# Squares summed on VectorE, a first round of four tiles, and a last norm through PSUM in a six-layer fp32 block chain

## The chip, the cores and the metric

The kernel runs on one core of a Trainium2 chip. A core has a matrix engine (TensorE, PE in the profile; PEld is its weight load), VectorE (DVE), ScalarE (ACT), GpSimd (POOL) and a queue engine for transfers (SyncE, SP). Data lie in SBUF; matrix products arrive in PSUM, in eight banks of 512 fp32 columns. The metric is the device time of one launch in microseconds (us), the median of several runs.

## What is computed

A chain of residual blocks over 512 tokens of width 1024, all in fp32. The first half has a hybrid mixer, a convolution mixer and two gated MLPs. The second half, where the change lies, is this (each branch is normed before and after):

```python
for i in range(2):
    h = rmsnorm(x, norm_mixer_pre[i])
    m = diff_attention(h, ...) if i == 0 else short_conv(h, ...)
    x = x + rmsnorm(m, norm_mixer_post[i])
    h = rmsnorm(x, norm_mlp_pre[i])
    x = x + rmsnorm(square(relu(h @ w_up)) @ w_down, norm_mlp_post[i])
# rmsnorm(x, g) = x * rsqrt(mean(x * x) + 1e-6) * g
```

## The kernel before

Activations are kept transposed: channels on the 128 partitions, the 512 tokens along the row. A vector of 1024 channels is eight blocks (k = 0 to 7, `KB` = 8) of 128 x 512. `h` is the residual stream, `m` the output of the current branch.

**Tiles.** Each weight matrix is streamed as tiles of 128 x 1024. Tile n goes to slot n mod 4 (`RING` = 4) of `raw`; ScalarE makes its rounded part `whi` (`split_hi`, L290), VectorE the rest `wlo` (`split_lo`, L684), and TensorE multiplies in three passes, (whi, xh), (whi, xl), (wlo, xh), over the eight blocks: 24 matmuls of 512 columns for one tile, all at L1283, into PSUM bank j. `xh` and `xl` are the same split of the activations. The slot of tile n is split for tile n + 4 once tile n is done and, on VectorE, its result has been taken out of PSUM.

**Boundaries.** Between a branch and the next one lie four post-norms: attention to the first MLP ("da" to "mlp0"), first MLP to short convolution ("mlp0" to "sc"), short convolution to second MLP ("sc" to "mlp1"), and the last one, whose result is the output. At each, the squares of `m` are summed (GpSimd adds them into `acc`, TensorE sums over the partitions with a matrix of ones, L1334 and L1336), ScalarE makes `rrow` = rsqrt of it with Ln and Exp (L313, L315), and then for each block k VectorE computes m = m * g * rrow (L705) and h = h + m (L709), ScalarE computes xh = h * g' and the square of h (L303, L299), and VectorE xl = h * g' - xh (L690, `pre_lo`) one block later. GpSimd adds those squares into `acc` too (`sum_squares`, a copy at L1193 and adds at L1196), for the norm of the branch that follows.

**First round.** TensorE's first tiles of the branch that follows don't wait for all of `h`: `first_round` runs three tiles (`FIRST` = 3) together, block by block, each block when its `xl` is there (`x_ready`); all three end with block 7. Its first passes are at L1364, L1365 and L1368. Then comes `row_sum` (L1339, the sum of the squares for the next `rrow`), then the fourth tile alone, then all others by `tile`. What is scaled by the new `rrow` is only the result of a tile, so tiles can run ahead of it as far as PSUM banks and weight slots go.

**After the first round** the MLP's VectorE clears `m` (L1107), waits for `rrow`, and for every tile does relu and scale (`mr`, L1114), a square (`mh`, L1117), the rest `yl` (L1123, after ScalarE's `yh`, L644) and then the split of the next weights. In the short convolution VectorE only scales the tile (L696) before the split.

**Last norm.** `post_norm("mlp1")` on VectorE does m for all blocks and h for the odd ones; GpSimd adds the even ones (L1273). SP stores each block when it is done.

The order on every engine is the order of the code; engines meet only at semaphores.

Of the kernel before, what the change touches and what calls it, by code (L numbers as in the profile page):

```python
# [102 lines left out]
def build(nc, x_t, stream, w_glr, w_gate, vecs, consts, out_t):  # L103
    with ExitStack() as ctx:
# [136 lines left out]

        BY_PE = ("hyb", "da_post", "mlp0_post", "sc_post", "mlp1_post")
        ACC, at = {}, 0
        for n in SUM:
            if n != "lnvar":
                ACC[n] = at
                at += KB - (n in BY_PE)
        PRE = {"hyb": 0, "ff0": 1, "pw": 2, "ff1": 3, "da": 4, "mlp0": 5, "sc": 6, "mlp1": 7}
        POST = {"da": 0, "mlp0": 1, "sc": 2, "mlp1": 3}


        @block.sync
        def _(sp):
            for name in CREDITED:
                sp.sem_inc(s(name), CREDIT)
            sp.dma_start(vec[:], vecs).then_inc(small_in[0], 16)
            sp.dma_start(A["wgr"][:], w_glr).then_inc(s("wglr_in"), 16)
            for k in range(KB):
                sp.dma_start(h[:, k], x_t[k * P:(k + 1) * P, :]).then_inc(x_in[k], 16)
            for j in range(RING):  # L260
                if j == 2:
                    sp.dma_start(const[:], consts).then_inc(small_in[1], 16)
                    sp.dma_start(A["wg2"][0:17, :], w_gate).then_inc(small_in[2], 16)
                sp.dma_start(raw[:, j], stream[j]).then_inc(loaded[j], 16)

            with sp.Fori(1, NT // RING) as r:
                for j in range(RING):
                    sp.wait_ge(wlo_ready, r * RING + (j + 1 - RING))
                    sp.dma_start(raw[:, j], stream[bass.ds(r * RING + j, 1)].rearrange("a p c -> (a p) c"))\
                      .then_inc(loaded[j], 16)  # L270
            for k in range(KB):
# [10 lines left out]
        def _(act):  # L282
# [22 lines left out]

            def inv_rms(name, n, preload=True, bank=4):

# [6 lines left out]
                act.wait_ge(ln_ready, SUM[name] + 1)  # L314
                act.activation(rrow[:], lnb[:], ACT.Exp, scale=-0.5).then_inc(rrow_ready, 1)  # L315

# [306 lines left out]
            def to_m(t0, which):  # L623

                act.preload_act_table_set(LN_EXP)
                for k in range(KB):
# [3 lines left out]
                    split_hi(t)  # L630
                inv_rms(which + "_post", D, preload=False)

# [3 lines left out]
            def mlp(f, t0):  # L636
                name = f"mlp{f}"
                inv_rms(name, D)

# [37 lines left out]
        def _(dve):  # L677
# [19 lines left out]

            def post_norm(which):

                a = POST[which]  # L700
                following = {"da": "mlp0", "mlp0": "sc", "sc": "mlp1"}.get(which)
                dve.wait_ge(rrow_ready, SUM[which + "_post"] + 1)
                for k in range(KB):
                    q = 8 * a + k
                    dve.scalar_tensor_tensor(A["m"][:, k], A["m"][:, k], col("post", q), rrow[:], ALU.mult,  # L705
                                             ALU.mult).then_inc(post_t, 1)
                    if following or k % 2:
                        dve.wait_ge(post_t, q + 1)
                        dve.tensor_tensor(h[:, k], h[:, k], A["m"][:, k], ALU.add).then_inc(h_added, 1)  # L709
# [390 lines left out]
            for k in range(KB):  # L1100
                set_m(Tile(T_DO + k), k)
            post_norm("da")

            def mlp(f, t0):
# [32 lines left out]
                for k in range(KB):  # L1137
                    add_to_m(Tile(t0 + 56 + k), k)
                post_norm(name)

            mlp(0, T_MLP0)


# [33 lines left out]
            for k in range(KB):  # L1177
                set_m(Tile(T_SCO + k), k)
            post_norm("sc")
            mlp(1, T_MLP1)  # L1180


        @block.gpsimd
        def _(pool):
# [82 lines left out]
            with pool.Fori(1, 4) as pair:  # L1267
                pair_inputs(pair)
            for name in ("da_post", "mlp0", "mlp0_post", "sc", "sc_post", "mlp1", "mlp1_post"):
                sum_squares(name)  # L1270
            for k in range(0, KB, 2):
                pool.wait_ge(post_t, 8 * POST["mlp1"] + k + 1)
# [4 lines left out]
        def _(pe):  # L1277
# [52 lines left out]
            def row_sum(name, bank=4):  # L1330
# [6 lines left out]
                else:  # L1337
                    pe.wait_ge(acc_ready, ACC[name] + KB)
                    mm = pe.matmul(ps[:, bank], cst("ones"), acc[:], start=True, stop=True)  # L1339
# [15 lines left out]

            def first_round(t0, hi, lo, hi_ready, ready, base):

                pe.wait_ge(wlo_ready, t0.plus(FIRST - 1).count)
                pe.wait_ge(evac_done, t0.count - 1)
                w_h = [whi[:, j].rearrange("p (k n) -> p k n", k=KB) for j in range(FIRST)]  # L1360
                w_l = [wlo[:, j].rearrange("p (k n) -> p k n", k=KB) for j in range(FIRST)]
# [5 lines left out]
                for j in range(FIRST):  # L1367
                    pe.matmul(ps[:, j], w_h[j][:, 0], lo[:, 0], start=False, stop=False)  # L1368
                for k in range(1, KB):
                    pe.wait_ge(ready, base + (k + 1))  # L1370
                    for j in range(FIRST):
# [242 lines left out]
            mm.then_inc(sum_ready, 1)  # L1614
            first_round(Tile(T_PW2), yh, yl, yh_ready, y_ready, Y0["pw"])
            for j in range(FIRST, KB):
# [298 lines left out]
```

## Time and profile before

| | |
|---|---|
| time, median of 3 runs | 2538.07 us (2537.42 to 2538.41) |
| span of the profiled execution, first to last instruction | 2539.4 us (no other time of it is given) |
| TensorE busy | 94% of the span, 10332 matmuls |
| VectorE, ScalarE, GpSimd busy | 55%, 35%, 13% |
| mean granted clock of TensorE | 0.970 |
| transfers | 82 GB/s over the span |

The profile gives, for each instruction, its start, its length, and in brackets the idle time of its engine just before it with what ended that. The chain of waits is the path that ended last, followed back from the end. TensorE is the engine that is nearly always busy; the stretches in which it is not are the boundaries above. Matmuls overlap, so the time that one costs is the distance between starts, not its length.

### The profile page before, as it was taken

Reading aid. Unit: us, or ns where it says so; the run is one execution under the profiler, and the core shown is the slowest. Engines: PE = TensorE matmul, PEld = TensorE weight load, DVE = VectorE, ACT = ScalarE, POOL = GpSimd, SP = SyncE. Lnnn points to the kernel's source line nnn. Section 1 sums busy time; section 2 is a strip of 40 time slices with the busy share of each in tenths; the row PEclk is TensorE's granted clock in tenths of the full one; section 3 lists DMA queues with packets and bytes.
Section 4 is the critical chain, followed back from the end, with each engine's and each line's share of the span. In section 5 each row is a group of like instructions: output and inputs, shape, how many; then the busy total and the mean of one; then the engine's idle time right before and its main releaser. Section 6 shows DMA issues by size and latency. Waiting matters only on the chain.

```text
span 2539.4 us, 29423 instructions
## 1 busy us (share of the span) xinstructions
PE 2394.7 (94%) x10332; PEld 1886.7 (74%) x10332; DVE 1399.7 (55%) x1630; ACT 877.7 (35%) x1180; POOL 325.5 (13%) x263
## 2 busy tenths in 40 slices
PE   7999999999967589999999999899999899899997
PEld 6867788888744358888887666688888688688885
DVE  4344443444799955444454764845544754844554
ACT  4256432322534344232242444422222322422222
POOL 1001200000456510000012221200001101100002
PEclk9999999999987789999999999999999999999998
DMA  4211233333311113333233110233333233233331
GB/s 163 83 50 34 67 99 100 91 99 99 92 42 41 33 34 107 97 94 99 91 116 92 42 42 28 80 108 100 91 100 95 79 92 99 70 97 100 99 91 50
DMA packets 58129, 208.53 MB, mean 82 GB/s; under 512 B 6449, under 2 KB 6594, under 8 KB 57922
## 3 DMA queue, kind: packets, MB, share of 16 engines
q1 hardware_dynamic: 58050, 207.42, 27.2%
q8 instruction: 56, 0.92, 0.1%
q14 instruction: 23, 0.19, 0.0%
HBM read 205.30 MB, written 2.10 MB: 82 GB/s over the span
## 4 chain that ended last, share of the span: by engine, by line
PE 58%; DVE 6%; ACT 1%; issue 1%; POOL 0%; ACTq 0%
PE ps L1283 53%; PE ps L1650 2%; DVE h L709 1%; DVE m L705 1%; DVE xl L690 1%; DVE wlo L684 1%; PE ps L1673 1%; PE ps L1652 1%; ACT whi L290 1%; PE ps L1611 0%; PE ps L1663 0%; PE ps L1680 0%; DVE cv L933 0%; ACT sq L299 0%; DVE m L1097 0%
## 5 line engine op out<-in xcount | busy, mean ns | idle before, releaser
L1283 PE MATMUL ps<-xh,whi 128*128 128x512 f32 x1767 | 703.6, 398 | 16.8 <-DVE xl L690 13.8
L1283 PE MATMUL ps<-xl,whi 128*128 128x512 f32 x1767 | 689.9, 390 | 0.0
L1283 PE MATMUL ps<-xh,wlo 128*128 128x512 f32 x1767 | 689.9, 390 | 0.0
L684 DVE TENSOR_TENSOR wlo<-raw,whi 128x1024 fp32r<-128x1024 f32 x380 | 482.0, 1269 | 265.8 <-ACT whi L290 254.9
L290 ACT ACTIVATE whi<-raw 128x1024 fp32r<-128x1024 f32 x380 | 398.6, 1050 | 486.4 <-PE ps L1283 486.3
L1283 PE MATMUL ps<-yh,whi 128*128 128x512 f32 x1117 | 437.1, 391 | 0.0
L1283 PE MATMUL ps<-yl,whi 128*128 128x512 f32 x1117 | 434.8, 389 | 0.0
L1283 PE MATMUL ps<-yh,wlo 128*128 128x512 f32 x1117 | 434.8, 389 | 0.0
L1283 PEld LDWEIGHTS ps<-xh,whi 128*128 128x128 f32 x1767 | 333.4, 189 | 101.7 <-DVE xl L690 23.1
L1283 PEld LDWEIGHTS ps<-xl,whi 128*128 128x128 f32 x1767 | 333.1, 189 | 72.0 <-issue 5.1
L1283 PEld LDWEIGHTS ps<-xh,wlo 128*128 128x128 f32 x1767 | 332.9, 188 | 70.4
L1283 PEld LDWEIGHTS ps<-yh,whi 128*128 128x128 f32 x1117 | 210.0, 188 | 44.6 <-issue 1.0
L1283 PEld LDWEIGHTS ps<-yh,wlo 128*128 128x128 f32 x1117 | 209.9, 188 | 43.9
L1283 PEld LDWEIGHTS ps<-yl,whi 128*128 128x128 f32 x1117 | 209.9, 188 | 43.7 <-issue 0.7
L1193 POOL COPY acc<-sq 128x512 f32<-128x512 f32 x12 | 8.0, 668 | 1527.0 <-ACT sq L299 1527.0
L1091 DVE TENSOR_TENSOR m<-ps,m 128x512 f32 (+1 forms) x64 | 44.3, 692 | 183.7 <-PE ps L1283 183.7
L1196 POOL TENSOR_TENSOR acc<-acc,sq 128x512 f32<-128x512 f32 x79 | 113.4, 1436 | 206.4 <-ACT sq L299 205.7
L644 ACT ACTIVATE yh<-mr 128x512 f32 x64 | 40.5, 633 | 225.3 <-DVE mr L1114 225.3
L1586 PE MATMUL ps<-ub,dg 128*128 128x512 f32 x96 | 62.0, 814 | 59.4 <-issue 35.2
L1231 POOL TENSOR_TENSOR pa<-pa,pr 128x512 f32<-128x512 f32 x64 | 99.0, 1547 | 5.0
L489 ACT ACTIVATE yh<-th 128x512 f32 x44 | 27.8, 632 | 205.6 <-DVE th L873 205.6
L1114 DVE SCALAR_TENSOR_TENSOR mr<-ps,rrow 128x512 f32<-128x512 f32 x64 | 44.2, 691 | 96.6 <-PE ps L1283 94.3
(214 smaller groups left out, 2197.7 us busy)
## 6 DMA issues: line engine op xcount, KB each, us to landing
raw<-stream SPq DMA_DIRECT2D x384, 512.0 KB, 3.5
h<-x_t SPq DMA_DIRECT2D x8, 256.0 KB, 5.5
out_t<-h SPq DMA_DIRECT2D x8, 256.0 KB, 2.1
const<-consts SPq DMA_DIRECT2D x1, 1089.0 KB, 9.6
wgr<-w_glr SPq DMA_DIRECT2D x1, 512.0 KB, 3.7
vec<-vecs SPq DMA_DIRECT2D x1, 212.0 KB, 2.6
wg<-w_gate SPq DMA_DIRECT2D x1, 17.0 KB
```

What stands on the lines that cost most here:

```text
L290: act.activation(whi[:, a.slot], raw[:, a.slot], ACT.Copy).then_inc(whi_ready, 1)
L489: act.activation(block_of(yh, i * 2 + u), A["th"][:, u], ACT.Copy).then_inc(yh_ready, 1)
L644: act.activation(block_of(yh, i * 4 + j), A["mr"][:, j % 2], ACT.Square).then_inc(yh_ready, 1)
L684: dve.tensor_tensor(wlo[:, a.slot], raw[:, a.slot], whi[:, a.slot].bitcast(F32), ALU.subtract)\
L690: dve.scalar_tensor_tensor(xl[:, k], h[:, k], col("pre", 8 * PRE[name] + k), xh[:, k].bitcast(F32), ALU.mult, ALU.subtract).then_inc(x_rea ...
L1091: dve.tensor_tensor(block_of(A["m"], k), ps[:, t.slot], block_of(A["m"], k), ALU.add)\
L1114: dve.scalar_tensor_tensor(A["mr"][:, j % 2], ps[:, t.slot], 0.0, rrow[:], ALU.max, ALU.mult)\
L1196: pool.tensor_tensor(acc[:], acc[:], sq[:, k % 2], ALU.add).then_inc(acc_ready, 1)
L1231: pool.tensor_tensor(A["pa"][:, u], A["pr"][:, u * prods % 4] if m == 1 else A["pa"][:, u], product, ALU.add).then_inc(s("cv_padd"), 1)
L1283: mm = pe.matmul(out, lhs, rhs, start=first and n == 0, stop=last and n == 2)
L1586: mm = pe.matmul(ps[:, 5 + u], A["dg"][:, u, k], A["ub"][:, u, k:k + T], start=k == 0, stop=k == TAPS_PE - 1)
L1650: pe.matmul(ps[:, b, 0:kv], A["dq"][r, e, 0, u * P:(u + 1) * P], A["dq"][r, e, 1, 0:kv], start=True, stop=True)
```

## The change

- `post_norm` sums the squares of `h` on VectorE (`sq_sum`), for "mlp0", "sc" and "mlp1": seven adds, the first of two squares at once, in place of GpSimd's copy and seven adds. GpSimd keeps the squares of `m`. `square_block` waits for the new count.
- `first_round` takes the number of tiles (4 in these three branches), keeps blocks 6 and 7 for the end (`tail` = 1) and runs them tile by tile, so that the four tiles end one after the other; `row_sum` follows the second of them.
- The explicit loads of ScalarE's function table in `to_m` (four) and before Ln at "mlp0", "sc" and "mlp1" (three) are gone.
- The last norm is a function of its own: ScalarE writes `rrow` into PSUM bank 5, VectorE reads it there, writes the scaled m of five blocks into PSUM banks 6 and 7 and adds it to h from there; GpSimd adds the other three blocks (0, 3, 6) instead of four.

```diff
@@ square_block
-                    act.wait_ge(acc_ready, ACC[name] + k - 1)
+                    act.wait_ge(acc_ready, ACC[name] + (max(k - 2, 1) if name in BY_DVE else k - 1))
@@ to_m
-                act.preload_act_table_set(LN_EXP)
...
-                inv_rms(which + "_post", D, preload=False)
+                inv_rms(which + "_post", D, preload=False, out=ps[:, 5] if which == "mlp1" else None)
@@ VectorE
+            def sq_sum(name, k):
+                dve.wait_ge(sq_ready, SQ[name] + k + 1)
+                if k == 1:
+                    dve.wait_ge(sum_ready, SUM[name])
+                    dve.tensor_tensor(acc[:], sq[:, 0], sq[:, 1], ALU.add).then_inc(acc_ready, 1)
+                else:
+                    dve.wait_ge(acc_ready, ACC[name] + k - 1)
+                    dve.tensor_tensor(acc[:], acc[:], sq[:, k % 2], ALU.add).then_inc(acc_ready, 1)
@@ post_norm, in the loop over k
-                    if following and k:
+                    if k:
                         pre_lo(following, k - 1)
-                if following:
-                    pre_lo(following, KB - 1)
+                    if k >= 2:
+                        sq_sum(following, k - 1)
+                pre_lo(following, KB - 1)
+                sq_sum(following, KB - 1)
+            def last_norm():
+                a = 8 * POST["mlp1"]
+                dve.wait_ge(rrow_ready, SUM["mlp1_post"] + 1)
+                for k in range(KB):
+                    n = LAST_DVE.index(k) if k in LAST_DVE else 0
+                    if n >= 2:
+                        dve.wait_ge(h_added, 8 * 3 + n - 1)
+                    t = A["m"][:, k] if k in LAST_POOL else ps[:, 6 + n % 2]
+                    dve.scalar_tensor_tensor(t, A["m"][:, k], col("post", a + k), ps[:, 5], ALU.mult,
+                                             ALU.mult).then_inc(post_t, 1)
+                    if k in LAST_DVE:
+                        dve.wait_ge(post_t, a + k + 1)
+                        dve.tensor_tensor(h[:, k], t, h[:, k], ALU.add).then_inc(h_added, 1)
@@ first_round
-                for k in range(1, KB):
+                for k in range(1, KB - 1 - tail):
                     pe.wait_ge(ready, base + (k + 1))
-                    for j in range(FIRST):
+                    for j in range(tiles):
+                        passes(ps[:, j], w_h[j][:, k], w_l[j][:, k], hi[:, k], lo[:, k], False, False)
+                for j in range(tiles):
+                    for k in range(KB - 1 - tail, KB):
+                        if j == 0:
+                            pe.wait_ge(ready, base + (k + 1))
                         mm = passes(ps[:, j], w_h[j][:, k], w_l[j][:, k], hi[:, k], lo[:, k], False, k == KB - 1)
-                        if k == KB - 1:
-                            mm.then_inc(tile_done, 1)
+                    mm.then_inc(tile_done, 1)
+                    if name and j == 1:
+                        row_sum(name)
@@ mlp on TensorE ("sc" likewise)
-                first_round(Tile(t0), xh, xl, xh_ready, x_ready, 8 * PRE[name])
-                row_sum(name)
-                tile(Tile(t0 + FIRST), FIRST, xh, xl)
+                first_round(Tile(t0), RING, xh, xl, xh_ready, x_ready, 8 * PRE[name], name, 1)
```

Two places, as the instructions stand in the program. VectorE at the boundary from "mlp0" to "sc", from the add of block 2, before:

```order
L709 TENSOR_TENSOR h<-h,m 128x512
L690 SCALAR_TENSOR_TENSOR xl<-h,vec,xh 128x512
L705 SCALAR_TENSOR_TENSOR m<-m,vec,rrow 128x512
L709 TENSOR_TENSOR h<-h,m 128x512
L690 SCALAR_TENSOR_TENSOR xl<-h,vec,xh 128x512
L705 SCALAR_TENSOR_TENSOR m<-m,vec,rrow 128x512
```

and now:

```order
L720 TENSOR_TENSOR h<-h,m 128x512
L693 SCALAR_TENSOR_TENSOR xl<-h,vec,xh 128x512
L706 TENSOR_TENSOR acc<-sq 128x512
L717 SCALAR_TENSOR_TENSOR m<-m,vec,rrow 128x512
L720 TENSOR_TENSOR h<-h,m 128x512
L693 SCALAR_TENSOR_TENSOR xl<-h,vec,xh 128x512
L709 TENSOR_TENSOR acc<-acc,sq 128x512
L717 SCALAR_TENSOR_TENSOR m<-m,vec,rrow 128x512
```

One add of squares now stands between the `xl` of a block and the m of the next but one.

VectorE at the last norm, from the last tile's evacuation, before:

```order
L1091 TENSOR_TENSOR m<-ps,m 128x512 x4
L705 SCALAR_TENSOR_TENSOR m<-m,vec,rrow 128x512 x2
L709 TENSOR_TENSOR h<-h,m 128x512
L705 SCALAR_TENSOR_TENSOR m<-m,vec,rrow 128x512 x2
L709 TENSOR_TENSOR h<-h,m 128x512
```

and now:

```order
L1119 TENSOR_TENSOR m<-ps,m 128x512 x4
L737 SCALAR_TENSOR_TENSOR m<-m,vec,ps 128x512
L737 SCALAR_TENSOR_TENSOR ps<-m,vec,ps 128x512
L741 TENSOR_TENSOR h<-ps,h 128x512
L737 SCALAR_TENSOR_TENSOR ps<-m,vec,ps 128x512
L741 TENSOR_TENSOR h<-ps,h 128x512
L737 SCALAR_TENSOR_TENSOR m<-m,vec,ps 128x512
```

Every instruction of VectorE now has one operand in PSUM, and five adds of h stand on it instead of four.

## Rows read from the trace of the kernel before

**Rows 1.** Chain of waits at "mlp0" to "sc": start us, us, what.
```profile
1971.22 0.76 DVE m L705
...
1993.68 4.39 PE ps L1283 x18
1998.07 0.86 PE ps L1339 x2
1998.93 157.84 PE ps L1283 x696
```

**Rows 2.** VectorE and GpSimd there, in order of time: start us, us, instruction.
```profile
1977.46 0.74 DVE L690 SCALAR_TENSOR_TENSOR xl<-h,vec,xh 128x512 fp32r<-128x512 f32 x1
1978.12 0.74 DVE L705 SCALAR_TENSOR_TENSOR m<-m,vec,rrow 128x512 f32<-128x512 f32 x1
...
1978.89 1.85 POOL L1196 TENSOR_TENSOR acc<-acc,sq 128x512 f32<-128x512 f32 x1 [1.91 <-ACT sq L299]
1978.89 0.69 DVE L709 TENSOR_TENSOR h<-h,m 128x512 f32<-128x512 f32 x1
...
1979.50 1.78 DVE L690 SCALAR_TENSOR_TENSOR xl<-h,vec,xh 128x512 fp32r<-128x512 f32 x1
```

**Rows 3.** TensorE's restart there, in order of time.
```profile
1973.60 0.77 PE L1364 MATMUL ps<-xh,whi 128*128 128x512 f32 x1 [3.71 <-ACT xh L303]
1974.16 0.63 PE L1365 MATMUL ps<-xh,wlo 128*128 128x512 f32 x1
1974.59 0.63 PE L1364 MATMUL ps<-xh,whi 128*128 128x512 f32 x1
```

**Rows 4.** Stretches of 1 us: busy by engine; PEclk is the third last number.
```profile
40.00:41.00 1.00, 1.00 (x3) 0.78 (x3) 1.00 (x2) 0.00 (x0) 0.00 (x0) 0.50 0.00 0
...
1613.00:1614.00 1.00, 0.62 (x2) 0.07 (x1) 1.00 (x2) 0.29 (x1) 0.13 (x1) 0.86 0.00 0
...
1978.00:1979.00 1.00, 0.75 (x3) 0.67 (x4) 0.97 (x3) 0.82 (x2) 0.11 (x1) 0.74 0.00 0
```

**Rows 5.** TensorE's restart at "da" to "mlp0", and from the sum to the fifth tile.
```profile
1609.74 0.64 PE L1364 MATMUL ps<-xh,whi 128*128 128x512 f32 x1 [3.71 <-ACT xh L303]
...
1632.27 3.47 DVE L1107 MEMSET m<- 128x4096 f32 x1 [0.80 <-issue]
...
1634.05 1.02 PE L1339 MATMUL ps<-acc,const 128*128 128x512 f32 x2
...
1636.84 0.69 DVE L1114 SCALAR_TENSOR_TENSOR mr<-ps,rrow 128x512 f32<-128x512 f32 x1 [1.10 <-ACT rrow L315]
...
1639.29 1.23 DVE L684 TENSOR_TENSOR wlo<-raw,whi 128x1024 fp32r<-128x1024 f32 x1
...
1640.57 0.50 PE L1283 MATMUL ps<-xh,whi 128*128 128x512 f32 x1
```

**Rows 6.** The same in "sc": ScalarE's Ln and VectorE's first split.
```profile
1998.96 0.60 ACT L313 ACTIVATE lnb<-ps 128x512 f32<-128x512 f32 x1 [4.46 <-PE ps L1339]
...
2001.21 1.23 DVE L684 TENSOR_TENSOR wlo<-raw,whi 128x1024 fp32r<-128x1024 f32 x1
```

**Rows 7.** Two idle spells of TensorE elsewhere, in order of time.
```profile
39.47 0.52 PE L1283 MATMUL ps<-xh,whi 128*128 128x512 f32 x1 [1.92 <-DVE gk L733]
...
1545.84 0.66 PE L1663 MATMUL ps<-const,da 128*128 128x128 f32 x4 [1.71 <-DVE da L1045]
```

**Rows 8.** VectorE at the last norm: its first and its last rows there.
```profile
2524.75 1.42 DVE L705 SCALAR_TENSOR_TENSOR m<-m,vec,rrow 128x512 f32<-128x512 f32 x2 [3.17 <-ACT rrow L315]
...
2535.18 1.64 DVE L709 TENSOR_TENSOR h<-h,m 128x512 f32<-128x512 f32 x1
```

**Rows 9.** VectorE and GpSimd in the convolution mixer, in order of time.
```profile
816.39 0.68 DVE L941 TENSOR_TENSOR cv<-ps,cv 128x512 f32 x1
...
816.87 1.27 POOL L1231 TENSOR_TENSOR pa<-pr 128x512 f32<-128x512 f32 x1 [10.32 <-ACT pr L523]
...
816.99 1.69 DVE L943 TENSOR_TENSOR odd<-pa,odd 128x512 f32<-128x512 f32 x1
```

More of the change, by code:

```diff
@@ L242, in build @@
         BY_PE = ("hyb", "da_post", "mlp0_post", "sc_post", "mlp1_post")
+        BY_DVE = ("mlp0", "sc", "mlp1")
+        ADDS = {n: KB - (n in BY_PE or n in BY_DVE) for n in SUM if n != "lnvar"}
         ACC, at = {}, 0
[L244 to L247, printed above, removed]
+        for n in ADDS:
+            ACC[n] = at
+            at += ADDS[n]
         PRE = {"hyb": 0, "ff0": 1, "pw": 2, "ff1": 3, "da": 4, "mlp0": 5, "sc": 6, "mlp1": 7}
         POST = {"da": 0, "mlp0": 1, "sc": 2, "mlp1": 3}
+        SQ = {n: (SUM[n] - (SUM[n] > 3)) * KB for n in SUM if n != "lnvar"}
+        LAST_POOL = (0, 3, 6)
+        LAST_DVE = tuple(k for k in range(KB) if k not in LAST_POOL)
         @block.sync
@@ L304, in pre_block, with inv_rms @@
                 square_block(name, k, h[:, k])
-            def inv_rms(name, n, preload=True, bank=4):
+            def inv_rms(name, n, preload=True, bank=4, out=None):
                 if preload:
@@ L314, in inv_rms @@
                 act.wait_ge(ln_ready, SUM[name] + 1)
-                act.activation(rrow[:], lnb[:], ACT.Exp, scale=-0.5).then_inc(rrow_ready, 1)
+                act.activation(rrow[:] if out is None else out, lnb[:], ACT.Exp, scale=-0.5).then_inc(rrow_ready, 1)
             def inv_rms_col(n, bank=5):
@@ L696, in scaled, with post_norm @@
                 dve.tensor_tensor(dst, ps[:, bank], rrow[:], ALU.mult).then_inc(evac_done, 1)
-            def post_norm(which):
+            def sq_sum(name, k):
[6 more added lines that the diff above has]
+                    dve.tensor_tensor(acc[:], acc[:], sq[:, k % 2], ALU.add).then_inc(acc_ready, 1)
+            def post_norm(which, following):
                 a = POST[which]
-                following = {"da": "mlp0", "mlp0": "sc", "sc": "mlp1"}.get(which)
                 dve.wait_ge(rrow_ready, SUM[which + "_post"] + 1)
@@ L1101, in _ @@
                 set_m(Tile(T_DO + k), k)
-            post_norm("da")
+            post_norm("da", "mlp0")
             def mlp(f, t0):
@@ L1178, in _ @@
                 set_m(Tile(T_SCO + k), k)
-            post_norm("sc")
+            post_norm("sc", "mlp1")
             mlp(1, T_MLP1)
+            last_norm()
         @block.gpsimd
@@ L1268, in _ @@
                 pair_inputs(pair)
-            for name in ("da_post", "mlp0", "mlp0_post", "sc", "sc_post", "mlp1", "mlp1_post"):
+            for name in ("da_post", "mlp0_post", "sc_post", "mlp1_post"):
                 sum_squares(name)
-            for k in range(0, KB, 2):
+            for k in LAST_POOL:
                 pool.wait_ge(post_t, 8 * POST["mlp1"] + k + 1)
@@ L1354, in col_sum, with first_round @@
                 mm.then_inc(colsum_ready, 1)
-            def first_round(t0, hi, lo, hi_ready, ready, base):
-                pe.wait_ge(wlo_ready, t0.plus(FIRST - 1).count)
+            def first_round(t0, tiles, hi, lo, hi_ready, ready, base, name=None, tail=0):
+                pe.wait_ge(wlo_ready, t0.plus(tiles - 1).count)
                 pe.wait_ge(evac_done, t0.count - 1)
-                w_h = [whi[:, j].rearrange("p (k n) -> p k n", k=KB) for j in range(FIRST)]
-                w_l = [wlo[:, j].rearrange("p (k n) -> p k n", k=KB) for j in range(FIRST)]
+                w_h = [whi[:, j].rearrange("p (k n) -> p k n", k=KB) for j in range(tiles)]
+                w_l = [wlo[:, j].rearrange("p (k n) -> p k n", k=KB) for j in range(tiles)]
                 pe.wait_ge(hi_ready, base + 1)
-                for j in range(FIRST):
+                for j in range(tiles):
                     pe.matmul(ps[:, j], w_h[j][:, 0], hi[:, 0], start=True, stop=False)
```

29 lines of the change are left out of this document (13 added, 16 removed).

## The prediction

> **What bounds the kernel now.** I read the chain of waits first. It is TensorE's tiles nearly throughout: after "mlp0" to "sc", for instance, 696 matmuls run in one piece of 157.84 us, 0.227 us each [rows 1]. What is not TensorE is the boundaries. There the chain starts with the first m (1971.22, call such a start T) and comes back to TensorE only at 1993.68, T + 22.5, with the last 18 of the first round's matmuls, then the sum of squares (done at 1998.93, T + 27.7), then the fourth tile [rows 1]. So VectorE sets the pace of a boundary, and TensorE waits for its `xl` block by block.
>
> The timeline of VectorE and GpSimd says why. From one start to the next VectorE needs 0.66 us for `xl`, 0.77 for m and 0.61 for h, 2.04 for a block. But the next `xl`, which began at 1979.50 while GpSimd's add of 1978.89 ran, took 1.78 instead of 0.74, until just after that add ended at 1980.74; and GpSimd's add took 1.85 [rows 2], against 1.27 for one that nothing held [rows 9]. The two exclude each other: whichever comes second waits. Over the eight blocks that makes T + 22.5 out of what would be T + 16.
>
> **VectorE at the three inner boundaries.** GpSimd's copy and seven adds go (hidden on GpSimd, dear by the waits that they cause). Seven adds of about 0.61 come onto VectorE. A block costs 2.04 + 0.61 = 2.65. The first `xl` starts at T + 2.8, the second ends at T + 5.6, that of block 5 at T + 16.2, of block 6 at T + 18.9, of block 7 at T + 20.1 (behind the add of block 6), and the last add at T + 20.8. ScalarE, with two instructions a block against VectorE's four, keeps up; the looser wait in `square_block` lets it square block 2 after the first add, 1.3 after h, in time for an add 3.4 after h. What is late next is TensorE.
>
> **TensorE's first round.** Four tiles are 96 matmuls, as three and then the fourth were: the work is the same, only more of it can run while `xl` is being made. It restarts at T + 2.38 (1973.60) at 1.2 GHz: starts 0.43 apart [rows 3]. The clock is back at 2.4 GHz at about 1978.5 here and 1613.3 at "mlp0", by the granted shares 0.74 and 0.86 of those microseconds [rows 4], so the low stretch from the restart is 4.9 us here and 3.5 at "mlp0" (restart 1609.74 [rows 5]); it costs half of itself. Before, VectorE's pace hid that; now it is on the path. Block 0: 2.38 + 12 x 0.227 + 1.8 = T + 6.9 at "mlp0", T + 7.6 at "sc". Each further block takes 12 x 0.227 = 2.72, more than VectorE's 2.65, and each `xl` is there before it is wanted (block 1 5.6 against 6.9, block 5 16.2 against 17.8, block 7 20.1 against 21.2): TensorE doesn't wait again. The sum comes after 72 more matmuls, 16.4 us: it starts at T + 23.3 and T + 24.0, its `acc` there since 20.8, and is done 1.02 later, at T + 24.3 and T + 25.0, instead of T + 27.7 (1634.05 + 1.02 at "mlp0" [rows 5]).
>
> **What waits for the sum.** Only half of the old cover stands behind the sum, 12 matmuls (2.7 us) instead of 24 (5.5). At "mlp0" the fifth tile started at 1640.57, right behind the end of its `wlo` (1639.29 + 1.23), 5.5 us after the sum: Ln, Exp, mr, square, `yl`, then the split [rows 5]. That chain is untouched, so the fifth tile starts at T + 24.3 + 5.5 = 29.8 instead of 33.2: 3.4 us won, and TensorE stands idle for 2.9 us before it, which it didn't. The clearing of m (3.47 us, 0.8 behind VectorE's last piece [rows 5]) ends at T + 25.1, 0.6 before the new `rrow`: hidden; without that cover it costs the difference. "mlp1" repeats it: 3.4. In "sc" the chain is shorter: the first split ended at 2002.44, 3.5 after the sum [rows 6]. Now T + 28.5, while TensorE is free at 27.6; before, the fifth tile began at 1998.93 + 24 x 0.227, T + 33.2: 4.6 won, 0.9 of idling.
>
> **The clock in the new idling.** A wait of 1.92 us at 39.47 was followed by 1.2 GHz in the next microseconds, one of 1.71 at 1545.84 was not [rows 4, 7]. 2.9 us is longer than either, so I expect a fall in both MLPs, and none in "sc" (0.9). Its price by the low stretches above is between nothing and half of 4.9, 2.5; I take 1.5 each, 3.0 lost.
>
> **Table loads.** Seven loads go. ScalarE idled for 4.46 us before the Ln at "sc" [rows 6], so the load before it was covered by TensorE's wait, and in `to_m` the matmuls of the tile cover it: 0. The Trainium skill's page ScalarE: Activation LUTs (What ACT_TABLE_LOAD costs) has 1.28 us and a drain of 1.38 for a switch; seven on the path would be another 18.6 us. The idle row says that they were not on it.
>
> **The last norm.** Before: 2524.75 to 2535.18 + 1.64, 12.1 us for twelve instructions, with h at 1.64 while GpSimd adds [rows 8]. A VectorE add with one operand in PSUM (816.39, 0.68 long) and GpSimd's (816.87, 1.27, its free length) ran over each other, while the next one with both in SBUF took 1.69 [rows 9]. So now the two don't hold each other: 3 x 0.66 + 5 x (0.77 + 0.61) = 8.9, 9.0 to the end of the last; GpSimd's block 6 ends 0.1 before. That is 3.1 won, less up to 0.7 because the last two stores are issued together (their landing isn't in a row): I take 2.5. VectorE writing to PSUM isn't in the trace; by the reads (0.68 against 0.69 [rows 2, 9]) it costs nothing, and I allow 0.1 either way for each. The page VectorE: DVE Perf Modes (The TRN2 errata) gives an instruction with its source in PSUM 62 cycles more than one from SBUF; 13 x 0.065 = 0.8 us, so 1.7 won instead of 2.5. The row of 0.68 speaks against it.
>
> **Sum.** 3.4 + 4.6 + 3.4 + 2.5 - 3.0 = 10.9 us: the profiled execution's 2539.4 would be 2528.5, the median 2538.07 becomes 2527.2 us.
>
> **Rivals.**
> - The clock stays up in the MLPs' idling (the 1.71 row speaks for it): 3.0 more won, 2524.2. 12%.
> - The PSUM operands don't free VectorE in the last norm: three waits of 1.0 come back, nothing won there, 2529.7. Rows 9 speak against. 8%.
> - The low stretches are longer, each like the one at "sc" or worse: 1 us more at three restarts and both idles, 2531. 7%.
> - Slower: VectorE's long instructions aren't GpSimd's doing. Then the seven adds lie on top: the last `xl`, before at T + 24.1 (22.5 and one more `xl`), comes at T + 27.5 or later; 9 matmuls and the sum after it give T + 30.6, 2.9 later, for the MLPs, and in "sc" T + 34.1 against 33.2; nothing is won at the end. 2538.1 + 2.9 x 2 + 0.9 = 2544.8. It decides once the last `xl` is later than about T + 24.5. The overlaps in rows 2 and 9 speak against it. 3%.
> - It does nothing, since something I don't see (a wait in the steady part, a transfer) takes the gain back: 2538. 3%.
>
> **How the numbers follow.** The forecast has 67%. The range must keep 8 in 10: forecast with its ends (clock price 0 to 2.5 each, stores 0 to 0.7) and the first two rivals, 2523.5 to 2530.5. A measurement tells about 0.2% (5 us) from no change: all but the last two rivals, and a part of the longer stretches, are below 2533. Faster 0.93, same 0.04, slower 0.03.
>
> **What would show it.** In the new profile: VectorE's m, h and xl at the inner boundaries all near 0.7, the last `xl` at T + 20; TensorE without waits from its second block on; the sum done near T + 24.3 and 25.0; then an idle of some 2.9 us before the fifth tile in both MLPs, 0.9 in "sc", with 1.2 GHz after the first two; GpSimd's three last adds at 1.27 and VectorE's last norm 9 us long. The prediction is wrong if `xl` of block 5 comes after T + 18, if the fifth tile waits for anything but `wlo`, or if the last norm's instructions exceed 0.8 us.

## The result, and the profile after

The changed kernel takes 2523.33 us (median of 4 runs, 2523.05 to 2525.89) against 2538.24 of the kernel before in the same comparison (2537.42 to 2540.85). The ratio is 0.9939, with a 95% interval of 0.9928 to 0.9951. The forecast was 2527.2 with a range of 2523.5 to 2530.5: the sign is right, the size is 3.9 us short, and the time lies 0.17 us below the range. The profiled execution of after has a span of 2521.3 us, before's 2539.4.

I read the chain of waits first, at "mlp0" to "sc" as in [rows 1]. Columns: start us, us, what.

```profile
1963.13 0.76 DVE m L717
1963.91 0.70 DVE h L720
...
1970.07 16.35 PE ps L1312 x72
1986.42 0.87 PE ps L1368 x2
...
1989.56 1.24 DVE wlo L687
1990.79 0.12 issue
1990.92 152.63 PE ps L1312 x672
```

With T = 1963.13, VectorE is in the chain only for its first m and h, up to the sum. TensorE then works from its restart to the sum without a wait: the 72 matmuls in one piece end at T + 23.3, the sum at T + 24.2 (before T + 27.7). Then comes one new stop: the fifth tile starts at T + 27.8, released by `wlo`.

Why VectorE has dropped out is seen in its instructions of that boundary, grouped by shape (line, engine, operation, count; busy us, mean ns; idle before):

```profile
L717 DVE SCALAR_TENSOR_TENSOR m<-m,vec,rrow 128x512 f32<-128x512 f32 x8 | 6.0, 746 | 0.3 <-ACT rrow L319 0.3
L693 DVE SCALAR_TENSOR_TENSOR xl<-h,vec,xh 128x512 fp32r<-128x512 f32 x8 | 6.0, 745 | 0.0
L720 DVE TENSOR_TENSOR h<-h,m 128x512 f32<-128x512 f32 x8 | 5.5, 692 | 0.3
L709 DVE TENSOR_TENSOR acc<-acc,sq 128x512 f32<-128x512 f32 x6 | 4.1, 685 | 0.0
```

All of them, and the first `acc` with 683 ns, 31 in all, have their short length. The 1.78 of [rows 2] is gone, and so is GpSimd, which has no instruction between 1957 and the end of the boundary. VectorE now does seven instructions more and is done 4 us sooner: `xl` of block 7 ends at T + 20.1.

In "mlp0" (T = 1601.28) the stretch from the sum to the fifth tile, which answers [rows 5], reads in order of time:

```profile
1622.80 3.47 DVE L1135 MEMSET m<- 128x4096 f32 x1 [0.80 <-issue]
...
1624.42 1.02 PE L1368 MATMUL ps<-acc,const 128*128 128x512 f32 x2
...
1627.21 0.69 DVE L1142 SCALAR_TENSOR_TENSOR mr<-ps,rrow 128x512 f32<-128x512 f32 x1 [0.94 <-PE ps L1312]
...
1629.65 1.22 DVE L687 TENSOR_TENSOR wlo<-raw,whi 128x1024 fp32r<-128x1024 f32 x1
...
1630.93 0.50 PE L1312 MATMUL ps<-xh,whi 128*128 128x512 f32 x1 [2.71 <-DVE wlo L687]
...
1631.65 0.63 PE L1312 MATMUL ps<-xh,wlo 128*128 128x512 f32 x1
```

The sum starts at T + 23.1, TensorE is out of work at T + 26.9, and the fifth tile starts at T + 29.65 after 2.71 us of idling. `mr` begins 2.79 us after the sum's start, just as in before (1634.05 to 1636.84 [rows 5]): the chain behind the sum is as long as it was, though the row of `mr` names PE as what ended its wait. The matmul of 1631.65 takes 0.63 instead of 0.39: the clock has fallen. The microseconds say the same (busy by engine; PEclk is the third last number, 0.50 is 1.2 GHz):

```profile
1630.00:1631.00 1.00, 0.07 (x1) 0.07 (x1) 1.00 (x2) 0.00 (x0) 0.00 (x0) 1.00 0.00 0
1631.00:1632.00 1.00, 1.00 (x3) 0.84 (x4) 0.96 (x2) 0.39 (x1) 0.00 (x0) 0.66 0.00 0
1632.00:1633.00 1.00, 1.00 (x4) 0.74 (x3) 0.73 (x2) 1.00 (x2) 0.00 (x0) 0.50 0.87 176
...
1635.00:1636.00 1.00, 1.00 (x6) 0.83 (x5) 0.74 (x2) 0.82 (x2) 0.00 (x0) 1.00 0.74 94
```

What this costs stands in the chain. The piece of 1440 matmuls of "mlp0" is 1.55 us longer in after (first row) than in before (second row):

```profile
1630.93 328.31 PE ps L1312 x1440
```
```profile
1640.57 326.76 PE ps L1283 x1440
```

The difference lies in the first 5 us of the piece. There after gets 15 matmuls done at a granted clock of 0.66, and before 22 at 1.00; seven matmuls of 0.227 us are 1.6 us. The next 64 us hold 284 matmuls in both.

The last norm, answering [rows 8 and 9], starts at 2509.24. VectorE and GpSimd there:

```profile
2509.24 0.75 DVE L737 SCALAR_TENSOR_TENSOR m<-m,vec,ps 128x512 f32<-128x512 f32 x1 [3.14 <-ACT ps L319]
2509.91 0.75 DVE L737 SCALAR_TENSOR_TENSOR ps<-m,vec,ps 128x512 f32<-128x512 f32 x1
2510.07 1.26 POOL L1302 TENSOR_TENSOR h<-h,m 128x512 f32<-128x512 f32 x1 [7.39 <-DVE m L737]
2510.70 0.69 DVE L741 TENSOR_TENSOR h<-ps,h 128x512 f32<-128x512 f32 x1
...
2517.56 0.69 DVE L741 TENSOR_TENSOR h<-ps,h 128x512 f32<-128x512 f32 x1
```

GpSimd's add runs at 1.26 beside VectorE's 0.75 and 0.69. The norm is 9.0 us long instead of 12.1.

**Stage by stage.** T1 to T4 are the starts of the first m at "da" to "mlp0", "mlp0" to "sc", "sc" to "mlp1", and at the end. The differences are the stages' lengths, and the span less T4 is the end.

| kernel | T1 | T2-T1 (mlp0) | T3-T2 (sc) | T4-T3 (mlp1) | end | sum of the four |
|---|---|---|---|---|---|---|
| before | 1607.36 | 363.86 | 189.44 | 364.09 | 14.63 | 932.02 |
| after | 1601.28 | 361.85 | 184.30 | 361.81 | 12.07 | 920.03 |
| gain | 6.1 | 2.0 | 5.1 | 2.3 | 2.6 | 12.0 |

So 12.0 us of the spans' 18.1 lie where the change is; 6.1 lie ahead of T1, where the only difference is one table load that is gone. That part is taken up with experiments 4 and 5.

### The profile page after: what moved, and what is told of

It reads as the page before. It is cut to its first block, busy times and chain, and to the rows that moved or that the text cites. A ratio compares the mean times of both kernels' runs of the same rounds, so it can differ in the third digit from the quotient of the medians.

```text
span 2521.3 us, 29407 instructions
## 1 busy us (share of the span) xinstructions
PE 2385.3 (95%) x10332; PEld 1885.5 (75%) x10332; DVE 1386.8 (55%) x1652; ACT 869.1 (34%) x1173; POOL 287.0 (11%) x238
## 3 DMA queue, kind: packets, MB, share of 16 engines
q1 hardware_dynamic: 58050, 207.42, 27.7%
## 4 chain that ended last, share of the span: by engine, by line
PE 60%; DVE 3%; ACT 2%; issue 1%; POOL 0%; ACTq 0%; DVEq 0%
PE ps L1312 54%; PE ps L1685 2%; DVE wlo L687 1%; PE ps L1708 1%; ACT whi L294 1%; PE ps L1687 1%; PE ps L1646 0%; PE ps L1698 0%; PE ps L1715 0%; DVE cv L961 0%; ACT sq L303 0%; PE ps L1393 0%; PE ps L1394 0%; DVE m L1125 0%; DVE h L875 0%
## 5 line engine op out<-in xcount | busy, mean ns | idle before, releaser
L1225 POOL TENSOR_TENSOR acc<-acc,sq 128x512 f32<-128x512 f32 x58 | 79.6, 1373 | 179.6 <-ACT sq L303 178.9
L493 ACT ACTIVATE yh<-th 128x512 f32 x44 | 27.8, 632 | 205.6 <-DVE th L901 205.6
```

What stands on the lines that cost most here:

```text
L493: act.activation(block_of(yh, i * 2 + u), A["th"][:, u], ACT.Copy).then_inc(yh_ready, 1)
L1225: pool.tensor_tensor(acc[:], acc[:], sq[:, k % 2], ALU.add).then_inc(acc_ready, 1)
```

## The experiments

All are timed beside runs of the kernel before on the same chip (e1 to e4: 2538.24 us, 27 runs; e5 to e8: 2536.73, 11 runs; e9 to e11: 2542.22, 7 runs). The four stages are from each kernel's profile, in the order of the table above.

**1. Only the VectorE sums (before + this).**

```diff
-            for name in ("da_post", "mlp0", "mlp0_post", "sc", "sc_post", "mlp1", "mlp1_post"):
+            for name in ("da_post", "mlp0_post", "sc_post", "mlp1_post"):
                 sum_squares(name)
...
+                    if k >= 2:
+                        sq_sum(following, k - 1)
+                pre_lo(following, KB - 1)
+                sq_sum(following, KB - 1)
```

> Of the change, only the squares summed by VectorE (first round of three tiles, table loads and last norm as before). Boundary theory: the last xl ends 20.1 us after the first m of a boundary instead of 24.1, TensorE (9 matmuls a block, 2.05 us, against VectorE's 2.65) still waits for VectorE, the sum is done at 23.3 instead of 27.7, and the whole fourth tile (5.5 us) still covers the chain behind it: fifth tile at 28.8 instead of 33.2 in both MLPs, 28.6 in the short convolution, no idle spell and no fall of the clock. 4.4 + 4.5 + 4.4 = 13.3 us less than before, about 2525. Rival, that the staggered round of four is where the gain is: under 6 us less, above 2532.

Measured: 2527.08 us (2525.49 to 2530.05), ratio 0.9958 (0.9945 to 0.9972). Stages 360.26, 185.86, 360.25, end 14.62: 11.0 us below before. TensorE in "mlp0" (T = 1602.71), its last wait for `xl` and its sum:

```profile
1621.60 0.50 PE L1311 MATMUL ps<-xh,whi 128*128 128x512 f32 x1 [0.32 <-DVE xl L694]
...
1625.84 1.02 PE L1367 MATMUL ps<-acc,const 128*128 128x512 f32 x2
```

The sum starts at T + 23.13, where after's starts too, and is done at T + 24.15. I had written T + 23.3; I had let block 7 begin when its `xl` was there, while 9 matmuls of block 6 were still ahead of it. The sums alone carry more than the whole inner gain: 3.6, 3.6 and 3.8, where the whole change has 2.0, 5.1 and 2.3. The fifth tile of an MLP starts at T + 29.65, exactly as in after, but with 24 matmuls of the fourth tile between sum and fifth tile TensorE doesn't stand still, and the clock stays up. Each MLP is 1.6 us shorter than after's.

**2. Only the four-tile round with staggered ends (GpSimd still sums).**

```diff
-                first_round(Tile(t0), xh, xl, xh_ready, x_ready, 8 * PRE[name])
-                row_sum(name)
-                tile(Tile(t0 + FIRST), FIRST, xh, xl)
+                first_round(Tile(t0), RING, xh, xl, xh_ready, x_ready, 8 * PRE[name], name, 1)
```

> Of the change, only the first round of four tiles with staggered ends (squares still on GpSimd). Boundary theory: xl of block 7 still ends at 24.1 after the first m; the sum is done at 27.2 instead of 27.7, the fifth tile of an MLP starts at 32.7 instead of 33.2 after 3 us of idling, which costs 1.5 us of clock each; the short convolution's fifth tile starts at 30.7 instead of 33.1. 2 x (0.5 - 1.5) + 2.4 = 0.4 us less than before, about 2537.8. Rival, that the round carries a gain of its own: 4 us or more less, under 2534.

Measured: 2537.39 us (2535.64 to 2541.19, 11 runs), ratio 0.9997 (0.9988 to 1.0006): no change. Stages 363.45, 187.54, 365.05, end 14.63. "sc" wins 1.9, "mlp0" 0.4, and "mlp1" loses 1.0. Both MLPs now idle for 2.7 us before the fifth tile. After the one in "mlp0" the clock stayed up, after the one in "mlp1" it fell. First the row and the microsecond in "mlp0":

```profile
1641.59 0.50 PE L1308 MATMUL ps<-xh,whi 128*128 128x512 f32 x1 [2.71 <-DVE wlo L688]
```
```profile
1642.00:1643.00 1.00, 1.00 (x6) 0.82 (x5) 0.83 (x2) 0.73 (x2) 0.00 (x0) 1.00 0.41 53
```

and then in "mlp1":

```profile
2192.59 0.50 PE L1308 MATMUL ps<-xh,whi 128*128 128x512 f32 x1 [2.72 <-DVE wlo L688]
```
```profile
2194.00:2195.00 1.00, 1.00 (x4) 0.81 (x3) 0.81 (x2) 0.85 (x1) 0.00 (x0) 0.50 0.65 233
```

The two stages differ by 1.6 us, which is the price of the fall. So the same idling is not followed by the same clock each time.

**3. Only the last norm, and 10. after with the last norm's operands back in SBUF.** e3 is before with after's `last_norm`. e10 is after with

```diff
-                inv_rms(which + "_post", D, preload=False, out=ps[:, 5] if which == "mlp1" else None)
+                inv_rms(which + "_post", D, preload=False, out=None)
...
-                    t = A["m"][:, k] if k in LAST_POOL else ps[:, 6 + n % 2]
-                    dve.scalar_tensor_tensor(t, A["m"][:, k], col("post", a + k), ps[:, 5], ALU.mult,
+                    t = A["m"][:, k]
+                    dve.scalar_tensor_tensor(t, A["m"][:, k], col("post", a + k), rrow[:], ALU.mult,
```

> Of the change, only the last norm through PSUM with three adds on GpSimd. Boundary theory: 2.6 us less than before, about 2535.6, all of it in the last 12 us. If the 2.8 us of gain that the boundaries don't account for hang on this part, 5.4 less.

> The changed kernel with one thing undone: in the last norm the products m and the row rrow lie in SBUF, not in PSUM. The split of the blocks between GpSimd (0, 3, 6) and VectorE stays. The output is the same. After's last stage is 12.07 us, before's 14.63. Theory (an instruction of VectorE with both inputs in SBUF and one of GpSimd keep each other waiting, and the operands in PSUM take that away): VectorE's thirteen instructions wait for GpSimd's three of 1.3 to 1.4 us, the last stage is 14.3 to 15.0 us. Rival (the gain is only that VectorE takes five blocks and GpSimd three instead of four and four): the last stage stays at 12.1 to 12.6 us. All before the last stage as after.

Measured: e3 takes 2537.16 us (2534.05 to 2538.5, 11 runs), ratio 0.9989 (0.998 to 0.9998), its end is 12.07 us long and its other stages are before's within 0.2. e10 takes 2530.13 us (2525.59 to 2534.48), ratio 0.9952 (0.9935 to 0.9968), and its end is 14.41 long. That "all before the last stage" would be as in after didn't hold for e10: its other stages are 362.76, 184.75 and 361.89, in sum 1.4 longer, with the same code; the low stretch after the restart in its "mlp0" was longer, and the sum there is done at T + 25.05 instead of 24.16. VectorE's rows at the last norm of e10, and then GpSimd's first:

```profile
2518.29 1.42 DVE L735 SCALAR_TENSOR_TENSOR m<-m,vec,rrow 128x512 f32<-128x512 f32 x2 [3.17 <-ACT rrow L319]
2519.74 1.63 DVE L739 TENSOR_TENSOR h<-m,h 128x512 f32<-128x512 f32 x1
2521.30 0.74 DVE L735 SCALAR_TENSOR_TENSOR m<-m,vec,rrow 128x512 f32<-128x512 f32 x1
2522.07 0.69 DVE L739 TENSOR_TENSOR h<-m,h 128x512 f32<-128x512 f32 x1
```
```profile
2519.12 1.70 POOL L1300 TENSOR_TENSOR h<-h,m 128x512 f32<-128x512 f32 x1 [7.41 <-DVE m L735]
```

The only difference between e10 and after is where m and `rrow` lie (and the wait for a free bank that goes with it). VectorE's add takes 1.63 where it meets GpSimd's (three times) and 0.69 where it doesn't, and GpSimd's takes 1.70 instead of 1.26. Three meetings of 0.94 make the norm 11.8 us long instead of 9.0. At the end of the kernel 2.34 of that shows, of the 2.56 us that after won there; the split of five blocks and three accounts for the other 0.2. The Trainium skill, SBUF — State Buffer (Who interferes with whom), says that a VectorE instruction with two inputs in SBUF contends with a GpSimd instruction that reads SBUF, and that one with at most one such input, outside the two-port modes, doesn't; these two traces agree (1.63 against 0.69).

**4. Only the table loads dropped, and 5. after once more, unaltered.**

```diff
-                act.preload_act_table_set(LN_EXP)
...
-                inv_rms(name, D)
+                inv_rms(name, D, preload=False)
```

> Of the change, only the seven table loads left out. Covered-loads theory: within 0.5 us of before, 2538. Rival, that a load holds ScalarE for longer than its row and this is the gain that the boundaries don't account for: about 2.8 us less, 2535.4.

> The changed kernel itself, unaltered, beside the runs below and with more runs of before. The parts read from its first profile sum to 12.1 us (3.6 + 5.3 + 3.8 at the inner boundaries, 2.6 at the end, less 1.55 of clock in each MLP). If the 14.9 us of the first four runs against the median of before held 2.8 us of scatter, the ratio here comes out near 0.9952; if something outside the boundaries gives 2.8 us each time, near 0.9941.

Measured: e4 takes 2537.62 us (2534.63 to 2542.47, 11 runs), ratio 0.9998 (0.9988 to 1.0007). Stages 364.01, 189.43, 363.85, end 14.62, in sum 0.1 from before. So the seven loads cost nothing that shows; they were covered. e5 takes 2529.22 us (2524.57 to 2530.95, 5 runs), ratio 0.9967 (0.9954 to 0.998), so here the same kernel gains 7.5 us and not 14.9. Its stages are 361.86, 184.28, 361.76, 12.07: within 0.1 us of after's, each of them. What differs is T1, 1605.98 against 1601.28. The two executions part early, as the stretch from 20 to 50 us shows (PEclk is the third last number), first of before, then of after, then of e5:

```profile
20.00:50.00 30.00, 28.08 (x159) 23.77 (x160) 10.91 (x13) 8.64 (x12) 0.00 (x0) 0.89 0.34 105
```
```profile
20.00:50.00 30.00, 28.08 (x173) 24.51 (x172) 11.46 (x15) 9.44 (x12) 0.00 (x0) 1.00 0.39 123
```
```profile
20.00:50.00 30.00, 27.99 (x165) 24.50 (x166) 11.10 (x14) 8.83 (x12) 0.00 (x0) 0.94 0.35 113
```

The code of this stretch is the same in all three, and so is TensorE's busy time; the granted clock is 0.89, 1.00 and 0.94, and the number of matmuls that fitted in follows it. Over the 13 profiled executions T1 lies between 1601.0 and 1608.9, for kernels that are alike up to there but for one load. T1 follows the clock: added up from the granted shares, the time at 1.2 GHz ahead of T1 was 126 us in before, 113 in after, 119 in e5, and 109 to 130 in all 13. T1 less half of that time lies between 1543.8 and 1546.5 in all of them, 2.7 us apart where T1 itself is 7.9 apart.

The change has no part in it that shows. e4 has the same code ahead of T1 as after, and its 11 runs are no faster than before's 27. A run's span less the stages of its kernel gives an estimate of its T1: for the 27 runs of before 1600.9 to 1609.1 with a median of 1604.4, for all nine of after 1601.3 to 1609.1 with a median of 1604.1. The first four of after (1601.3, 1604.1, 1601.8 and 1601.3) came early by chance. Nine runs of after have a median of 2525.89 us, all 49 of before one of 2538.24: 12.3 us apart, near the 12.0 of the stages. Neither ratio that I had expected of e5 came out: by its interval its five runs lie above both, by their late T1 (median 1607.4).

**6. Filling the idle spell, and 7. three tiles in the MLPs.** Both take the idling before the fifth tile away. e6 adds work (12 more matmuls whose result nobody reads), e7 goes back to the old round in the MLPs and keeps the new one in "sc".

```diff
                 first_round(Tile(t0), RING, xh, xl, xh_ready, x_ready, 8 * PRE[name], name, 1)
+                for _ in range(12):
+                    pe.matmul(ps[:, 6], exact[:, 0:P], xh[:, 7], start=True, stop=True)
```
```diff
-                first_round(Tile(t0), RING, xh, xl, xh_ready, x_ready, 8 * PRE[name], name, 1)
+                first_round(Tile(t0), FIRST, xh, xl, xh_ready, x_ready, 8 * PRE[name])
+                row_sum(name)
+                tile(Tile(t0 + FIRST), FIRST, xh, xl)
```

> The changed kernel with twelve more matmuls of 512 columns, whose result nobody reads, on TensorE behind the first round of each MLP, in its idle spell of 2.9 us (12 x 0.227 = 2.7 us of work). Clock theory: TensorE is no longer idle there, the clock stays at 2.4 GHz, the fifth tile still starts 29.7 us after the first m, and each MLP is 1.55 us shorter: 3.1 us less than the changed kernel. Rival, that 1.55 us of longer matmuls at the start of the MLP have another cause (VectorE or transfers): the same time, or more by the fillers' work.

> The changed kernel with the first round of three tiles, the sum and then the fourth tile alone in both MLPs, as before; the short convolution keeps the round of four. Boundary theory: the fifth tile of an MLP at 28.9 instead of 29.7 after the first m and no idle spell: 2 x (0.8 + 1.55) = 4.7 us less than the changed kernel. Rival, that four tiles together are worth more because TensorE doesn't wait for VectorE: 1 us or more longer than the changed kernel.

Measured: e6 2522.68 us (2520.82 to 2531.34, 6 runs), ratio 0.9948 (0.9933 to 0.9962); stages 360.28, 185.20, 360.70, end 12.07. e7 2522.59 us (2520.45 to 2527.26, 5 runs), ratio 0.9947 (0.9934 to 0.9959); stages 360.28, 185.08, 360.22, end 12.07. TensorE in e6's "mlp0" (T = 1603.49), filler and fifth tile:

```profile
1630.29 2.91 PE L1772 MATMUL ps<-xh,exact 128*128 128x512 f32 x12
1633.17 0.50 PE L1312 MATMUL ps<-xh,whi 128*128 128x512 f32 x1
1633.50 0.40 PE L1312 MATMUL ps<-xl,whi 128*128 128x512 f32 x1
```

The fifth tile starts at T + 29.7, no sooner than in after, but its matmuls take 0.40 and 0.39 and the "mlp0" stage is 1.57 us shorter. Useless matmuls make the kernel faster. The loss in after's MLPs is thus the clock's fall and not the idling: the fifth tile can't start before its `wlo`, whether TensorE waits or works till then. In "mlp1" e6 wins only 1.1, and "sc" is 0.8 to 0.9 longer in both than in after. There the low stretch after the restart was longer: the granted clock of the ten microseconds from the restart in "sc" is 0.75 in e7 and 0.83 in after (e7's row below, then after's), 0.8 us of work at 2.4 GHz. e7's fifth tile in "mlp0" starts at T + 29.67, as in after and e1, and not at 28.9 as I had written. So e7 wins only the clock, 1.57 and 1.59 in its MLPs, and not the 0.8 beside it. The rows of the clock in "sc":

```profile
1963.67:1973.67 10.00, 10.00 (x34) 8.07 (x35) 9.86 (x16) 5.46 (x9) 0.00 (x0) 0.75 0.05 18
```
```profile
1965.50:1975.50 10.00, 10.00 (x37) 8.10 (x38) 9.86 (x16) 5.47 (x9) 0.00 (x0) 0.83 0.04 14
```

**8. The sum one tile earlier, m cleared by GpSimd, and 11. the sum alone.**

```diff
-                    if name and j == 1:
+                    if name and j == 0:
                         row_sum(name)
```

and in e8 only:

```diff
-                dve.memset(A["m"][:], 0.0).then_inc(s("m_zero"), 1)
...
+                if name in ("da_post", "sc_post"):
+                    pool.wait_ge(h_added, 8 * (POST[name[:-5]] + 1))
+                    pool.memset(A["m"][:], 0.0).then_inc(s("m_zero"), 1)
```

> The changed kernel with the sum of squares behind the first of the four tiles instead of the second, and m cleared by GpSimd instead of VectorE. Boundary theory: the sum is done 1.4 us earlier (22.8 after the first m), 18 matmuls (4.1 us) cover the chain of 5.5 us behind it, the idle spell shrinks to 1.5 us and the clock stays up: 2 x (1.4 + 1.55) + 0.9 in the short convolution = 6.8 us less than the changed kernel. Rival, that the clearing blocks VectorE or the clock falls all the same: 3.7 us less or fewer.

> The changed kernel with one thing altered: the row sum's matmul stands after the first tile of the staggered round instead of after the second, and the memset of m stays on VectorE (e8 moved both). The output is the same. Theory (in the MLPs VectorE's memset, which ends at T+25.0, is next once the sum comes sooner): in the two MLPs mr can't begin before T+25.0, against T+25.9 of after, so an idle spell of about 1.8 us stays, each of the two stages is 0.5 to 0.9 us shorter than after's 361.85 if the clock still falls after the idle spell, and about 2.4 if it doesn't; in the small stage, which has no memset of this size there, 0.9 us. Rival (the memset costs nothing, all of e8's 3.0 us in an MLP is the earlier sum): stages as e8's 358.9, 183.1, 359.4.

Measured: e8 2521.48 us (2517.95 to 2523.21, 5 runs), ratio 0.9936 (0.9923 to 0.9949); stages 358.88, 183.12, 359.41, end 12.07. e11 2517.21 us (2516.34 to 2521.63, 4 runs), ratio 0.9906 (0.9889 to 0.9922); stages 359.18, 183.03, 359.31, end 12.07. In sum that is 913.5 and 913.6, some 6.5 below after, for the 6.8 expected of e8. So the earlier sum does nearly all of it. Clearing m on VectorE costs 0.3 us in "mlp0", where `mr` starts only at the memset's end and the idle spell is 1.62 instead of e8's 1.35, and nothing in "mlp1" (-0.1), where the sum came 0.4 later. e11 in "mlp0" (T = 1606.26), VectorE's memset and mr, then TensorE's fifth tile, then its clock:

```profile
1627.78 3.47 DVE L1135 MEMSET m<- 128x4096 f32 x1 [0.80 <-issue]
1631.17 0.63 DVE L1142 SCALAR_TENSOR_TENSOR mr<-ps,rrow 128x512 f32<-128x512 f32 x1
```
```profile
1634.83 0.50 PE L1312 MATMUL ps<-xh,whi 128*128 128x512 f32 x1 [1.62 <-DVE wlo L687]
```
```profile
1635.00:1636.00 1.00, 1.00 (x5) 0.82 (x6) 0.96 (x2) 0.49 (x1) 0.00 (x0) 1.00 0.50 33
```

The fifth tile starts at T + 28.6, 1.1 sooner than in after, the idle spell is 1.62 instead of 2.71, and the clock stays up: 1.1 + 1.55 is the 2.7 us by which the stage is shorter. Of the branches that I had written down it is the one without a fall (2.4 expected). The rival's stages, those of e8, are as close: the two forecasts differed by 0.5 us in an MLP, and only the row of `mr` tells them apart in "mlp0".

**9. The first split ahead of the row's root** (e8 plus this, VectorE shown; ScalarE's half of the split moves ahead of Ln in the same way, and the first pass of the loop is written out).

```diff
+                split_lo(Tile(t0))
                 dve.wait_ge(rrow_ready, SUM[name] + 1)
...
-                        split_lo(t)
+                        if j or not first:
+                            split_lo(t)
```

> e8's kernel, and in the two MLPs the first weight pair that the fifth tile needs is split before the row's root instead of behind it: ScalarE's split stands ahead of Ln and Exp, VectorE's subtraction ahead of its wait for rrow. The output is the same. In e8's trace the fifth tile of the MLPs begins at T+28.27 and T+28.80 after an idle spell of 1.35 us, its last wait being the split. Theory (the chain behind the row sum, sum - Ln - Exp - mr - yl - split, sets the fifth tile): TensorE then waits only for mr, which ends near T+25.5, so the fifth tile begins as soon as the fourth ends, T+26.8 to 27.2, no idle spell; each of the two stages is 1.3 to 1.6 us shorter than e8's 358.88 and 359.41, the small stage and the last are as in e8 (183.1 and 12.07), the sum of the four stages is about 3 us below e8's. Rival A (VectorE's backlog, not the split, is next: mr of the later tiles comes late): the idle spell moves into the second round and the stages stay within 0.3 us of e8's. Rival B (splitting ahead delays Ln by ScalarE's 0.6 us for one block and nothing is gained beyond 0.7 us).

Measured: 2517.80 us (2515.44 to 2521.66, 4 runs), ratio 0.9914 (0.9898 to 0.9931); stages 357.24, 183.77, 358.07, end 12.07, in sum 911.2, 20.9 below before. VectorE in "mlp0" (T = 1602.50):

```profile
1625.62 1.23 DVE L694 TENSOR_TENSOR wlo<-raw,whi 128x1024 fp32r<-128x1024 f32 x1 [2.40 <-ACT whi L294]
1626.77 0.69 DVE L1149 SCALAR_TENSOR_TENSOR mr<-ps,rrow 128x512 f32<-128x512 f32 x1
```

The split ends at T + 24.35 and `mr` at T + 25.0, before TensorE is through with the fourth tile. Neither MLP has an idle spell any more, and the stages are 1.6 and 1.3 us shorter than e8's, as the theory has it. "sc" is 0.65 longer (its sum starts at T + 22.4 instead of 21.7, by the low stretch after the restart). By the stages e9 is 2.4 us ahead of e11; the medians, 2517.80 and 2517.21, can't tell the two apart. By the stages they are 8.9 (e9) and 6.4 us (e11) shorter than after.

## Why the prediction came out as it did

**VectorE at the inner boundaries: right.** The last `xl` ends at T + 20.1, to the tenth, a block takes 2.65, and the two engines' mutual waiting is what had made T + 24.1 of it. The rival by which VectorE's long instructions weren't GpSimd's doing is out: e1 moves the sums from GpSimd to VectorE, with the looser wait that goes with it, and nothing else, and wins 11.0 us. e10 brings the meeting back at the other end and loses 2.3.

**TensorE's round and the sum: right at "mlp0", too late by 0.9 in "sc".** Expected T + 24.3 and 25.0, found 24.2 and 24.2. In before the clock was back up 4.9 us after the restart in "sc"; in after it was so after 3.7, by the granted share of this microsecond (restart at 1965.50):

```profile
1969.00:1970.00 1.00, 1.00 (x5) 0.78 (x5) 0.97 (x2) 0.63 (x1) 0.00 (x0) 0.88 0.00 0
```

A low stretch of one execution isn't a constant of the place: e7's sum at the same place is done at T + 24.9. That term was 4.6 and measures 5.1 in this execution. With longer low stretches, nearer to the 4.9 us that I had assumed, e7, e6 and e10 have 4.4, 4.2 and 4.7, so the extra half microsecond is luck.

**What waits for the sum: right.** Idle spells of 2.71 and 2.7 (I had 2.9) and 0.86 (0.9), all released by `wlo`; the fifth tile at T + 29.65 for 29.8. VectorE's memset was covered, as said.

**The clock in the idling: right in kind and in price.** A fall in both MLPs, 1.55 us each for the 1.5 of the sum. e6, e7 and e2 put 1.6 on it in three ways. With the fall, "mlp0" wins 2.0 for the 1.9 expected and "mlp1" 2.3 (before's fifth tile there stood at T + 33.46, 0.25 later than in "mlp0", which I hadn't read).

**Table loads 0, last norm 2.5: right.** Measured 0 and 2.56, of which the norm won 3.06 and the stores gave 0.5 back. The rival on the PSUM operands is out by e3 and e10. The Trainium skill's page VectorE: DVE Perf Modes (The TRN2 errata), by whose longer PSUM row I had estimated 0.8 us as lost, doesn't hold for these forms, which have one source in PSUM and one in SBUF: the add takes 0.69 so, and 0.69 with both in SBUF where it doesn't meet GpSimd (e10).

**Where it failed: the step "How the numbers follow".** The time is 3.9 us below the forecast. Of that 1.1 is in the terms of the sum: the stages give 12.0 us for 10.9 forecast (2.0 and 2.3 for 1.9 each in the MLPs, 5.1 for 4.6, 2.56 for 2.5), and 2538.24 - 12.0 is 2526.2, well inside the range. The other 2.9 us came ahead of T1, where the change does nothing, and this is the step that failed: the range put the scatter between executions at nothing. Its ends are those of the clock's price and the stores, though the same step says that a measurement tells about 5 us; the three times of before that I had (2537.42 to 2538.41) lie within 1 us and don't show the scatter. The runs show it: T1 moved over 7.9 us among 13 profiles with the time at 1.2 GHz ahead of it, 27 runs of before lie between 2534.64 and 2542.88, and nine of after between 2523.05 and 2530.95 with a median of 2525.89, inside the range. That the first four lay so low is chance. The time alone would speak for the first rival (2524.2, the clock stays up); the trace, with its fall in both MLPs, rules it out. So the mechanisms held; by that spread of 7.9 us, I estimate that a range for four runs needed some 3 us more on either side.

What I hadn't asked is whether each part earns its place. The sums alone give 11.0 us and the last norm 2.6, in all 13.6. The four-tile round gives 1.6 in "sc" by after (0.7 to 1.1 by e6, e7 and e10, where the low stretch was longer) and takes 1.6 in each MLP, so that the three together come to 12.0.

## What to carry to other kernels

Where VectorE and GpSimd meet on operands in SBUF, look at the long instructions on both sides before moving work: here it paid to give the fast engine seven more instructions, or to put one operand in PSUM. When a first round is reordered so that a sum comes out sooner, ask what stands behind the sum: TensorE's work there covers a chain (root, scaling, split), and if the cover is cut below the chain's length the chain must be shortened with it, by taking the sum earlier still (e11) or what doesn't need the sum out of it (e9); or the cover stays (e7). And compare stages inside the trace rather than spans, since the stretch ahead of the change scattered here by 7.9 us, more than the change was worth in any one stage.

## What the runs showed of the hardware that I had not expected

- The stage lengths repeated to 0.1 us in after and e5, and to 0.9 us in e10, whose code is the same there, while the arrival at T1 moved over 7.9 us among 13 profiles. It followed the time at 1.2 GHz ahead of it (109 to 130 us), about half of which is delay.
- An idle spell of 2.7 us of TensorE was followed by 1.2 GHz in 7 of 8 cases (after, e5 and e10 twice each, e2 once of twice). Spells of 1.34 to 1.62 us (e8, e11, four cases) and of 0.86 were never followed by it. Each fall cost 1.55 to 1.6 us.
- The low stretch after the restart at a boundary is not the same from one execution to the next: the stage "sc" was 184.3 us long in after and e5 and 185.1 in e7, which has the same code there.
- Twelve superfluous matmuls before a late tile made "mlp0" 1.57 us faster than idling did, and "mlp1" 1.1.
